# Expert rows gathered by indirect DMA and expert outputs combined on GpSimd, in the mixture of a one-core decoder trunk

## What is computed

```
logits = h @ w_router                              # h: (256, 1024)
top_vals, top_idx = top_k(logits, 2); top_w = softmax(top_vals)
combine = sum(one_hot(top_idx, 8) * top_w, over the 2)
for e in range(8):                                 # w_gu[e]: (1024, 7168), w_down[e]: (3584, 1024)
    g, u = split(h @ w_gu[e], 2)
    out += combine[:, e] * ((silu(g) * u) @ w_down[e])
x = x + g2 * out                                   # g2: the layer's gate, one row of 1024
```

## Time and profile before

| | |
|---|---|
| median of 3 runs | 1721.69 us (1719.17 to 1723.15) |
| the profiled execution | 1717.87 us, of which the span of its instructions is 1716.0 us |
| PE busy | 1650.5 us, 96% of the span |
| DVE, ACT busy | 1393.5 us (81%), 1096.8 us (64%) |
| POOL busy | 0.2 us |
| DMA | 497.94 MB, mean 290 GB/s |

### The profile page before, as it was taken

The page is one execution under the profiler, slowest core; times in us unless marked ns, Lnnn a source line. Parts: engine busy times, 40 slices in busy tenths (PEclk is TensorE's granted clock), DMA queues, the critical chain, the costliest instruction groups (busy, mean ns, idle before and its releaser), DMA issues.

```text
span 1716.0 us, 25116 instructions
## 1 busy us (share of the span) xinstructions
PE 1650.5 (96%) x7709; PEld 1303.9 (76%) x7709; DVE 1393.5 (81%) x1573; ACT 1096.8 (64%) x1338; POOL 0.2 (0%) x4
## 2 busy tenths in 40 slices
PE   7988999999999989899999999999999999999996
PEld 2736777777778767688888888888888888888884
DVE  2675877775577685798998998998998998998995
ACT  2653434333455653677777777877787787777773
POOL 0000000000000000000000000000000000000000
PEclk9999999999999999999999999999999999999998
DMA  9785887874545123499999999999999999999991
GB/s 355 265 301 197 329 310 269 287 266 157 192 149 169 60 74 123 156 368 360 368 351 336 384 354 331 386 354 336 376 358 351 355 370 343 358 370 347 354 372 67
DMA packets 207238, 497.94 MB, mean 290 GB/s; under 512 B 18155, under 2 KB 20508, under 8 KB 207016
## 3 DMA queue, kind: packets, MB, share of 16 engines
q1 hardware_dynamic: 207144, 496.91, 80.3%
HBM read 495.78 MB, written 1.07 MB: 290 GB/s over the span
## 4 chain that ended last, share of the span: by engine, by line
PE 88%; DVE 6%; ACT 3%; issue 2%; DMA 1%; SPq 0%; DVEq 0%; ACTq 0%
PE acc L1589 26%; PE acc L1596 25%; PE acc L1590 25%; PE xb L1901 2%; PE xb L1867 2%; PE acc L1574 1%; PE xb L1626 1%; PE acc L1689 1%; DMA raw<-in_ada_w 1%; DVE cv L1356 1%; DVE w_lo L938 1%; PE acc L1995 1%; PE xb L1674 1%; PE xb L1890 1%; PE xb L1891 1%
## 5 line engine op out<-in xcount | busy, mean ns | idle before, releaser
L938 DVE TENSOR_TENSOR w_lo<-raw,w_hi 128x1024 fp32r<-128x1024 f32 x832 | 993.6, 1222 | 165.4 <-ACT w_hi L579 140.4
L579 ACT ACTIVATE w_hi<-raw 128x1024 fp32r<-128x1024 f32 x832 | 864.7, 1058 | 305.9 <-PE acc L1596 283.1
L1589 PE MATMUL acc<-w_hi,g_hi 128*128 128x512 f32 x896 | 354.3, 395 | 1.0 <-DVE g_lo L1535 1.0
L1590 PE MATMUL acc<-w_hi,g_lo 128*128 128x512 f32 x896 | 349.0, 390 | 0.0
L1596 PE MATMUL acc<-w_lo,g_hi 128*128 128x512 f32 x896 | 276.6, 390 | 0.1
L1596 PEld LDWEIGHTS acc<-w_lo,g_hi 128*128 128x128 f32 x896 | 168.0, 188 | 36.3 <-DVE w_lo L938 0.8
L1589 PEld LDWEIGHTS acc<-w_hi,g_hi 128*128 128x128 f32 x896 | 168.3, 188 | 34.5 <-issue 1.1
L1589 PE MATMUL acc<-w_hi,a_hi 128*128 128x512 f32 x464 | 185.4, 400 | 8.8 <-DVE a_lo L988 4.5
L1590 PEld LDWEIGHTS acc<-w_hi,g_lo 128*128 128x128 f32 x896 | 168.4, 188 | 33.2
L1590 PE MATMUL acc<-w_hi,a_lo 128*128 128x512 f32 x464 | 181.8, 392 | 0.0
L1589 PE MATMUL acc<-w_hi,e_hi 128*128 128x512 f32 x448 | 177.9, 397 | 0.0
(11 more groups left out here) (257 smaller groups left out, 1455.5 us busy)
## 6 DMA issues: line engine op xcount, KB each, us to landing
raw<-in_moe_w_gu SPq DMA_DIRECT2D x448, 512.0 KB, 5.9
raw<-in_moe_w_down SPq DMA_DIRECT2D x224, 512.0 KB, 5.4
raw<-in_ada_w SPq DMA_DIRECT2D x96, 512.0 KB, 6.3
raw<-in_ffn_w_gu SPq DMA_DIRECT2D x56, 512.0 KB, 5.7
raw<-in_ssm_w_in SPq DMA_DIRECT2D x40, 512.0 KB, 4.4
raw<-in_ffn_w_down SPq DMA_DIRECT2D x28, 512.0 KB, 5.2
raw<-in_ssm_w_out SPq DMA_DIRECT2D x16, 512.0 KB, 4.4
raw<-in_attn_w_qkv SPq DMA_DIRECT2D x12, 512.0 KB, 12.6
```

The lines of the kernel that those rows point to most:

```text
L579: act.activation(w_hi[:, w % SPLIT, :], raw[:, no % RAW, :], ACT.Copy).then_inc(hi_ready, 1)
L938: dve.tensor_tensor(w_lo[:, w % SPLIT, :], raw[:, no % RAW, :], r32(w_hi[:, w % SPLIT, :]), ALU.subtract).then_inc(raw_used, 1)
L1589: pe.matmul(o, l_hi[:, k, rows_], hi[:, col:col + HALF], start=new, stop=False)
L1590: pe.matmul(o, l_lo[:, k, rows_], hi[:, col:col + HALF], start=False, stop=False)
```

## The change

**Tokens in.** The normalized tokens `hm` are stored to a DRAM scratch `hm_scratch` by GpSimd (with a row of zeros at its end, written by SP). PE multiplies each expert's `pick` with the column `token` of token numbers, and DVE writes the rows as integers into `row_of`. GpSimd gathers 128 rows of 4 KB per expert by an indirect DMA into `g_rows` (`gather_rows`), and PE transposes them in three pieces (`turn_gathered`; G_BLOCKS: 4, 2 and 2 transposes). `t_hi` and `t_lo` are gone; `g_hi` and `g_lo` are now both split from the transposed piece.

**Outputs.** For experts 0 to 6 ACT copies the output as plain float32 into `yd`, and GpSimd stores it to `y_scratch` (512 KB). Only expert 7 keeps the scatter, outside the loop. When expert 6's output is stored, GpSimd gathers the two rows of each token (`place_of`) from `y_scratch` with four indirect DMAs, and multiplies, adds, scales by g2 and adds into `x` with ten operations on 128x1024. DVE adds expert 7's part at the end and signals `x_ready` before its `value_load` and `If`.

**Weights.** Gate and up tiles are now 1024 columns in one run, so each row is 4 KB (`mixture_source`, MIX_COLS). A group of 8 tiles holds only gates, only ups, or (the second) the last 512 gates and the first 512 ups. The gates wait in the SBUF tile `gate` for their ups (`mix_gates`, `mix_products`). An expert has 10 pieces instead of 16.

```diff
+    MIX_COLS = (0, 3 * TW, TW, FF + HALF, 2 * TW, FF + HALF + TW, FF + HALF + 2 * TW)
+    MIX_UP = {1: (0,), 3: (1, 2), 5: (3, 4), 6: (5, 6)}
+    G_BLOCKS = ((0, 4), (4, 6), (6, 8))
+    MIX_PIECES = FJ + len(G_BLOCKS)
+    def mixture_source(w_gu, w_down, s):
+        if s < FJ * KD:
+            gi, k = divmod(s, KD)
+            return w_gu[k * P:(k + 1) * P, MIX_COLS[gi]:MIX_COLS[gi] + TW]
...
                     if B.mixture and s == 2:
                         act.wait_ge(w_used, B.full(-1))
-                        act.activation(yd_hi[:, :], acc[2][:, :], ACT.Copy).then_inc(yd_hi_ready, 1)
+                        act.wait_ge(yd_free, 1 + STORED * B.rnd + rep(e, 1))
+                        act.activation(yd[:, :], acc[2][:, :], ACT.Copy).then_inc(acc_done[2], 1)
...
+            def mix_products(B, gi):
+                if gi not in MIX_UP:
+                    return
...
+                if gi == 3:
+                    dve.tensor_tensor(gate[:, HALF:3 * HALF], gate[:, HALF:3 * HALF], acc[q][:, :], ALU.mult).then_inc(acc_done[q], 1)
+                    return
+                for m, j in enumerate(MIX_UP[gi]):
+                    col = HALF if gi == 1 else m * HALF
+                    ins = dve.tensor_tensor(mix_hidden(j), mix_hidden(j), acc[q][:, col:col + HALF], ALU.mult)
...
-            def scatter_sum(c, t, hf, col, e=0):
...
+            def gather_rows(rnd, e):
+                if e:
+                    pool.wait_ge(xb_full, pc0["moe"] + rnd * ROUND_PIECES + FIRST_PIECES + MIX_PIECES * (e - 1))
+                pool.indirect_dma_start(g_rows[:, :], None, hm_dram[:, :],
+                                        bass.IndirectOffsetOnAxis(ap=row_of[:, e:e + 1], axis=0)).then_inc(ld_rows_of, 16)
+                pool.wait_ge(ld_rows_of, 16 * (EXPERTS * rnd + e + 1))
+                pool.sem_inc(rows_in, 1)
+                for e in range(STORED):
+                    pool.wait_ge(acc_done[2], pair_uses0[2] + rnd * EXPERTS + e + 2)
+                    pool.dma_start(y_dram[e * P:(e + 1) * P, :], yd[:, :]).then_inc(st_y, 16)
+                    pool.wait_ge(st_y, 16 * (STORED * rnd + e + 1))
+                    pool.sem_inc(yd_free, 1)
+                    if e + 2 < EXPERTS:
+                        gather_rows(rnd, e + 2)
...
+                for t in range(T):
+                    for q in range(2):
+                        own(pool.tensor_scalar(y_got[:, t, q, :], y_got[:, t, q, :], tw[:, t, 1 + q:2 + q], None, ALU.mult))
+                    own(pool.tensor_tensor(y_got[:, t, 0, :], y_got[:, t, 0, :], y_got[:, t, 1, :], ALU.add))
+                    own(pool.tensor_tensor(y_got[:, t, 0, :], y_got[:, t, 0, :], mod[:, MOD_SLOT[1][5], :], ALU.mult))
+                    own(pool.tensor_tensor(x[:, t, :], x[:, t, :], y_got[:, t, 0, :], ALU.add))
+                    pool.sem_inc(partial_ready, 1)
```

More of the change, by code:

```diff
@@ L295, in body_pieces @@
         for j in range(FJ):
-            after.setdefault(KD * (j + 1) + 3, []).extend(("h", j, t) for t in range(1 if mixture else T))
-        if mixture:
-            for n in range(2 * T):
-                after.setdefault(2 * KD + 4 + 2 * n, []).append(("scatter", n // 2, n % 2))
-            after.setdefault(3 * KD + 4, []).append(("put",))
-            for n in range(4):
-                after.setdefault(FJ * KD + 8 + 4 * n, []).append(("gather", n // 2, n % 2))
+            if mixture:
+                gi = MIX_GROUP[j]
+                after.setdefault(KD * (gi + 1) + 3 + 2 * MIX_UP[gi].index(j), []).append(("h", j, 0))
+            else:
+                after.setdefault(KD * (j + 1) + 3, []).extend(("h", j, t) for t in range(T))
+        if mixture:
+            for n in range(len(G_BLOCKS)):
+                after.setdefault(FJ * KD + 8 + 4 * n, []).append(("gather", n))
         else:
@@ L317, in build @@
     PIECES = {False: body_pieces(False), True: body_pieces(True)}
-    assert sum(len(v) for v in PIECES[True].values()) == 16
+    assert sum(len(v) for v in PIECES[True].values()) == MIX_PIECES and MIX_PIECES % 2 == 0
     assert sum(len(v) for v in PIECES[False].values()) == 2 * FJ + 12
@@ L1240, in body @@
                         split_lo(B.raw_no(s), B.spl + s, e)
-                    if B.mixture and s == 2:
-                        dve.wait_ge(yd_hi_ready, B.rnd * (EXPERTS + 1) + 1 + rep(e, 1))
-                        dve.tensor_tensor(yd_lo[:, :], acc[2][:, :], r32(yd_hi[:, :]), ALU.subtract).then_inc(acc_done[2], 1)
                     j, k = divmod(s, KD)
                     if 1 <= j <= FJ and k == 2:
-                        for t in range(B.tiles):
+                        if B.mixture:
+                            mix_products(B, j - 1)
+                        for t in range(0 if B.mixture else T):
                             q, _ = B.pair(j - 1, t)
-                            dve.wait_ge(gate_ready, gates(B, j - 1, t))
+                            dve.wait_ge(gate_ready, T * (j - 1) + t + 1)
                             dve.tensor_tensor(h[:, t, :], h[:, t, :], acc[q][:, HALF:2 * HALF], ALU.mult).then_inc(acc_done[q], 1)
@@ L1474, in _ @@
             own(dve.memset(slot_of[:, :, :], -1.0))
-            own(dve.memset(y_sum[:, :, :], 0.0))
-            own(dve.memset(r32(put[:, :, :]), 0.0))
+            own(dve.reduce_sum(token[:, 0:1], tri_strict, axis=AX.X))
+            for t in reversed(range(T)):
+                own(dve.tensor_scalar(token[:, t:t + 1], token[:, 0:1], -1.0, float(P - 1 + t * P - SEQ), ALU.mult, ALU.add))
             residual("wout", 0, mod[:, MOD_SLOT[1][2], :])
@@ L1543, in _ @@
+                dve.wait_ge(dve_step, done)
+                dve.sem_inc(x_ready, 1)
             experts(0)
@@ L1827, in body @@
                 e = B.e
[L1828 removed]
+                per = MIX_PIECES if B.mixture else 0
                 gu = (g_hi, g_lo) if B.mixture else (a_hi, a_lo)
@@ L1891, in scatter @@
                 pe.matmul(b[:, :], put[:, t, :], yd_lo[:, cols], start=False, stop=True).then_inc(xb_full, 1)
-            def gather(c, low, hf, e, per, rnd):
-                if low == 0 and hf == 0:
-                    pe.wait_ge(pick_ready, rnd * T * (EXPERTS + 1) + T + rep(e, T) + (T if per else 0))
-                b = open_piece(c, e, per)
-                src = t_lo if low else t_hi
-                for m in range(4):
-                    for t in range(T):
-                        mm = pe.matmul(b[:, m * P:(m + 1) * P], src[:, t, (4 * hf + m) * P:(4 * hf + m + 1) * P], pick[:, t, :],
-                                       start=t == 0, stop=t == T - 1)
-                mm.then_inc(xb_full, 1)
             ada_group_end, n = {}, 0
@@ L2042, in _, with slot_rows @@
             pe.matmul(b[:, 2 * EXPERTS:3 * EXPERTS], ones, msk[:, 1, :], start=False, stop=True).then_inc(xb_full, 1)
+            def slot_rows(c, first, end, picks0):
+                b = open_piece(c)
+                for e in range(first, end):
+                    pe.wait_ge(pick_ready, picks0 + T * (e + 1))
+                    for t in range(T):
+                        mm = pe.matmul(b[:, e:e + 1], r32(pick[:, e, t, :]), token[:, t:t + 1], start=t == 0, stop=t == T - 1)
+                mm.then_inc(xb_full, 1)
             def experts(rnd):
@@ L2055, in experts @@
                 pe.wait_ge(yd_lo_ready, rnd + 1)
-                for n in range(4):
-                    scatter(pc0["moe"] + rnd * ROUND_PIECES + 4 + 16 * EXPERTS + n, n // 2, n % 2, 0, 0)
+                for n in range(2 * T):
+                    scatter(first + FIRST_PIECES + MIX_PIECES * EXPERTS + n, n // 2, n % 2)
             experts(0)
```

276 lines of the change are left out of this document (182 added, 94 removed).

## The result

The changed kernel takes 1697.49 us in the median of 4 runs (1695.21 to 1701.34); the kernel before took 1722.42 us beside it (4 runs, 1719.17 to 1723.5). The ratio is 0.9865 with a 95% interval of 0.9847 to 0.9883. So the change saves 24.9 us where 28.8 were forecast. The profiled execution after took 1695.21 us with a span of 1693.4 us, 22.6 us less than the 1716.0 of before.

What follows compares the result with a forecast made beforehand. PE's instruction stream was taken to bound the mixture. Pieces -38.4, start +4.1 and +1.0, end -5.6, GpSimd's operations +10.1 sum to -28.8 us, from 1721.69 to 1693 us; range 1679 to 1704.

Steps and rivals of the forecast that it cites:

- Pieces, -38.4 us: Eight expert bodies: PE loses gathers, scatters and the put, gains transposes; net 4.8 us saved per expert, -38.4 us in all.
- Transfers cost nothing: Expert bodies: the ring and PE's work hide the DMA transfers, 45.1 MB in 118.7 us at 380 GB/s; counted at nothing.
- the thinnest cover: Expert bodies: DMA must sustain 380 GB/s for the whole gain, against 387 GB/s seen over 25 us.
- The rival in which DMA becomes the bound: Expert bodies: traffic stays at 357 GB/s, an expert takes 126.3 us, the kernel 1744 us; chance 0.06.
- Waits of GpSimd in the inner experts: Inner experts: GpSimd's output store and row gather, 4.4 to 5.9 us each, are hidden by some 85 us.
- GpSimd's ten operations, +10.1 us: Expert 7's body: 15.2 us of GpSimd arithmetic stop DVE's w_lo stream; PE's remaining wait is +10.1 us.
- the upper bound of 19: Expert 7's body: GpSimd's ten operations take 15.2 us in all, bounds 11.5 and 19 us.
- The rule named in the prediction: SBUF port pair: a two-SBUF-input DVE operation and a GpSimd operation reading SBUF exclude each other for their whole length.
- The first rival: Expert 7's body: GpSimd's arithmetic costs PE nothing, giving 1683 us; chance 0.27.
- Start of the mixture, +4.1 and +1.0 us: First pick to first tile: 10.2 us instead of 6.1, +4.1 us; plus 1.0 us for tiles at the lower clock.
- The clock term: Start of the mixture: PE nearly idle, so tiles run at the lower clock level; +1.0 us, bounds 0 and 3.5.
- End, -5.6 us: After the last tile: value_load, If and four operations leave the path to the output DMA; -5.6 us.

Runs made afterwards that it cites:

- e1: Changed kernel without GpSimd's ten operations, so the result lacks the outputs of experts 0 to 6; 1687.2 us, ratio 0.9799.
- e2: Changed kernel with gate and up tiles loaded in 2 KB rows again, products as before; 1699.28 us, ratio 0.9874.
- e4: Changed kernel with the scaling by g2 and the addition to x moved from GpSimd to DVE's end; 1694.81 us, ratio 0.9844.
- e6: Changed kernel with GpSimd's operations spread over body 7, the second tile's scaling and both additions to x moved to DVE; 1687.77 us, ratio 0.9808.
- e3: Changed kernel without the four warm matmuls ahead of expert 0's gathered rows; 1695.8 us, ratio 0.9856.
- e5: Changed kernel with two instead of three warm matmuls before the token products, three singles between them, none behind; 1697.29 us, ratio 0.9875.
- e7: Changed kernel with the edits of e5 and e6 together; 1688.65 us, ratio 0.9809.
- e10: e6 with DVE's place tables ahead of the second piece's row numbers and WARM_GATHER 2 instead of 4; 1689.94 us, ratio 0.9801.
- e9: e7 with DVE's place tables put ahead of the second piece's row numbers; 1685.7 us, ratio 0.9781.
- e8: Kernel before, with its last four operations and the output's signal put ahead of DVE's value_load and If; 1719.76 us, ratio 0.9994.

## Why the prediction was right, and where it was off

The time lay in the range, 4.5 us above the forecast. The main mechanisms, PE's work counted piece by piece and DVE's `w_lo` behind GpSimd's operations, were seen in their places; one term at the start was mis-sized, and two errors in another cancelled by luck. By its steps:

- **Pieces, -38.4 us: right.** Bodies 0 to 6 lost 34.4 us, 4.91 each, and body 7 without GpSimd's operations (e1) 4.8; the forecast was 4.8. Adding up PE's work piece by piece is enough where PE never waits.
- **Transfers cost nothing: right**, and the thinnest cover held: 375 to 385 GB/s in the windows of the six inner experts, and no wait of PE for a load. The rival in which DMA becomes the bound (1744 us) is refuted. The limit of about 358 GB/s that the Trainium skill gives (DMA: Bandwidth & Descriptors, Specifications) doesn't hold for this kernel on its one core. The longer landing (7.8 instead of 5.9 us) is no bottleneck, since e2's is 9.8 us at the same pace. What the forecast left open, whether the 4 KB rows are needed, e2 answers: they aren't.
- **Waits of GpSimd in the inner experts: hidden, right.** The windows with its stores and gathers are as long as forecast (118.6 to 118.7 us).
- **GpSimd's ten operations, +10.1 us: right as a cost (11.4), with two errors in the working that cancel; that the number fits so well is luck.** The operations take 36.0 us and not 15.2, above the upper bound of 19: a one-tensor operation was priced by ACT's 1.02 us and takes 3.5 to 4.7, a two-tensor one was bounded by 2.44 and takes 2.4 to 3.25. But they don't stop DVE for their whole length. DVE gets one `w_lo` through for each two-tensor operation (3.3 us against 1.22) and loses some 0.8 us, once, beside each one-tensor one. In body 7 DVE's busy time grew by 15.0 us against e1 (121.0 - 106.1), as if it had been stopped for the forecast's 15.2 us. The rule named in the prediction (the Trainium skill, SBUF — State Buffer, Who interferes with whom) agrees with the trace for two-tensor operations: the six `w_lo` end 1.1 us behind them. For one-tensor ones the trace doesn't bear it out: most `w_lo` beside them are at full speed, 1.2 us. The first rival (1683 us) is refuted by e1. What cost was in part the amount (four two-tensor operations fewer saved 7.6 us, e4) and in part the bunching (e6 against e4: one operation more, spaced, costs 0.5 us and not 3.7). A smaller slip: 15.2 us are 11 tiles and not 15, so DVE's spare time would be 1.9 us instead of 2.6.
- **Start of the mixture, +4.1 and +1.0 us: the step that was mis-sized, +10.0 us.** The terms named add up to 9.9 us and not to 10.2; the measured lead-in is 16.1. The gather was priced fairly (5.4, bounds 4.4 and 12; it took 4.2 from issue to landing). From the first pick to its issue 1.3 us were counted and 3.1 passed, and the turn took 3.9 instead of 3.2. The largest part, 4.9 us, the sum didn't have at all; it stands in PE's queue: behind the token products, which end before the rows land, come the warm matmuls, and at the lower clock they hold PE 5 us past the landing. The clock term was right in kind, but it fell on these matmuls, not on tiles. e3, e5, e7 and e10 show that this isn't simply freed: less filler gives 2.3 to 3.8 us in the lead-in (in e7 next to none) and costs 1.6 to 2.5 us in body 0. Only where the order on DVE was changed too (e9) is a part, 3.4 us, kept in the profile, and that is hardly more than the 2.9 us between e5 and e7.
- **End, -5.6 us: -4.9.** DVE's four rounds took 5.6 and not 6.2 us, and the issue came 6.5 us earlier; 1.6 us come back at the end of the span, and e8, which changes nothing but the order, shows the same 1.6. The forecast counted the branch as gone, where it had only moved.

What stays open: when and why the clock falls. In nine of the eleven profiles with the new lead-in it falls 3.6 to 4.7 us after the first pick, while PE is at the token products; in e5 and e9 it falls over 11 us after the pick; in the two with the old lead-in (before and e8) it doesn't fall there. e9 and e7 differ in DVE's order alone, and their lead-ins are at full and at half level, but e5 and e7 differ in nothing up to there, and theirs differ too. So the execution decides at least in part, and no run here singles out what PE did before. Nor was it tried to leave the adding to ACT, which is busy only 96 of 118.6 us.

## What to carry to other kernels

Where one engine is busy without a gap, take work off it and count it piece by piece; the gain came as counted here, since the other engines and the DMA kept up. Work put on GpSimd beside a busy DVE isn't free, and it costs less when single stalls stay within what the ring between the engines holds: ten operations in one bunch cost 11.4 us, six in one bunch 3.7, seven spaced out over the body 0.5. When a wait on a DMA is added, read what is queued on each engine between the issue and the use, and what PE's clock does meanwhile: here the transfer took 4.2 us and the gap grew by 10. And before a difference of 3 us between two profiles is put down to an edit, look for two profiles that share the code of that stretch.
